# A hybrid convolution decoder step on one core: late spills cut in halves, quadrant loads moved behind them, merge sigmoids staged in PSUM

## What is computed

```python
z = rmsnorm(h, norm_g)
a_val, a_glu, a_gate, b_h, b_c, b_b, b_gate, m_a, m_b = split(z @ w_in)   # nine blocks of 1024 columns
c_a = layernorm(causal_dwconv(buf_a, a_val * sigmoid(a_glu), conv_a_w) + conv_a_b)   # width 31
y_a = silu(c_a) * silu(a_gate)
y_b = b_b * causal_dwconv(buf_b, b_c * b_h, conv_b_w) * silu(b_gate)                # width 3
merged = sigmoid(m_a) * (y_a @ w_pa) + sigmoid(m_b) * (y_b @ w_pb)
y = rmsnorm(h + merged @ w_out)
```

## Time and profile before

| what | us |
|---|---|
| median of 3 runs (1175.93 to 1176.99) | 1176.33 |
| the profiled execution's own time | 1175.6 |
| its span, first to last instruction | 1173.8 |
| TensorE matmul busy in it | 1055.5 |
| late units n = 2 to n = 10 (to slot 4) | 233.03 |

### The profile page before, as it was taken

How to read it: one execution, slowest core, us unless ns; L and a number is a source line. 1 busy time by engine, 2 the same in 40 slices (tenths; PEclk the granted TensorE clock), 3 DMA queues, 4 the chain that set the end, 5 groups by cost and what they waited for, 6 DMA issues and landing times.

```text
span 1173.8 us, 19871 instructions
## 1 busy us (share of the span) xinstructions
PE 1055.5 (90%) x7948; PEld 1024.7 (87%) x7948; DVE 762.7 (65%) x816; ACT 460.1 (39%) x694; POOL 601.6 (51%) x451
## 2 busy tenths in 40 slices
PE   4868999999999999999998888895966986997997
PEld 4868999999999999999998888895966976996885
DVE  5635979899999999898845436330661384646333
ACT  7334343433434444344344444461541252222221
POOL 2155666565656565665745555543754564545000
PEclk8888999999999999999999999888988988998999
DMA  7446575666656667565688879988669877764220
GB/s 258 107 118 139 129 196 128 181 153 164 164 146 171 157 162 173 143 174 144 160 245 223 236 207 271 282 238 285 168 190 282 226 187 213 198 235 163 91 90 37
DMA packets 217583, 212.24 MB, mean 181 GB/s; under 512 B 10799, under 2 KB 171055, under 8 KB 216452
## 3 DMA queue, kind: packets, MB, share of 16 engines
q1 hardware_dynamic: 192724, 165.88, 44.5%
q0 software_dynamic: 24768, 45.10, 21.4%
HBM read 131.83 MB, written 35.00 MB: 142 GB/s over the span
## 4 chain that ended last, share of the span: by engine, by line
PE 64%; DMA 12%; issue 5%; DVE 4%; POOL 4%; ACT 3%; SPq 2%; ACTq 0%; DVEq 0%; POOLq 0%
PE pp L1816 55%; PE pp L1968 8%; POOL wop L837 4%; DMA m_spill<-big 3%; DMA ring<-in_w_in_dram 2%; DMA ring<-ring 2%; DMA big<-mb_spill 2%; DVE big L1529 2%; DMA ga_spill<-big 1%; DVE big L1531 1%; SPq L433 1%; ACT xop L932 1%; ACT wop L906 1%; DMA mb_spill<-big 1%; DMA big<-yb_spill 1%
## 5 line engine op out<-in xcount | busy, mean ns | idle before, releaser
L1816 PE MATMUL pp<-xop,wop 128*128 128x262 f32 (+1 forms) x7224 | 913.6, 289 | 82.9 <-ACT big L1060 61.2
L1816 PEld LDWEIGHTS pp<-xop,wop 128*128 128x128 f32 x7224 | 906.4, 194 | 88.0 <-issue 82.9
L837 POOL TENSOR_TENSOR wop<-ring,wop 128x512 fp32r<-128x512 f32 (+1 forms) x262 | 455.2, 1745 | 367.5 <-ACT wop L906 367.1
L906 ACT ACTIVATE wop<-ring 128x512 fp32r<-128x512 f32 (+1 forms) x262 | 182.0, 698 | 271.5 <-PE pp L1816 258.1
L1512 DVE TENSOR_TENSOR big<-big,pp 128x524 f32<-128x524 f32 (+1 forms) x43 | 29.9, 694 | 121.6 <-PE pp L1816 120.8
L1432 DVE SCALAR_TENSOR_TENSOR big<-big,cst 128x513 f32<-128x513 f32 x112 | 104.7, 935 | 0.6
L1968 PE MATMUL pp<-xop,wop 128*128 128x512 f32 x384 | 91.3, 400 | 6.7 <-DVE wop L1766 6.7
L1968 PEld LDWEIGHTS pp<-xop,wop 128*128 128x128 f32 x384 | 73.4, 192 | 24.3 <-issue 6.9
L1443 DVE SCALAR_TENSOR_TENSOR spare<-big,tap_sum,spare 128x512 f32<-128x512 f32 x112 | 83.7, 748 | 0.3
L1432 DVE SCALAR_TENSOR_TENSOR spare<-big,cst,spare 128x512 f32<-128x512 f32 x112 | 83.6, 746 | 0.0
L1347 DVE TENSOR_TENSOR xop<-big,xop 128x2064 fp32r<-128x2064 f32 (+1 forms) x21 | 54.0, 2592 | 41.6 <-ACT xop L932 41.5
(11 more groups left out here) (119 smaller groups left out, 674.4 us busy)
## 6 DMA issues: line engine op xcount, KB each, us to landing
ring<-in_w_in_dram SPq DMA_DIRECT2D x249, 256.0 KB, 3.5
ring<-ring POOLq DMA_DIRECT2D x172, 256.0 KB, 4.5
big<-c_spill SPq DMA_DIRECT2D x16, 516.0 KB, 6.7
ring<-in_w_pb_dram SPq DMA_DIRECT2D x28, 256.0 KB, 4.2
ring<-in_w_pa_dram SPq DMA_DIRECT2D x28, 256.0 KB, 3.6
big<-yb_spill SPq DMA_DIRECT2D x5, 1032.0 KB, 11.3
big<-ya_spill SPq DMA_DIRECT2D x5, 1032.0 KB, 11.8
yb_spill<-big SPq DMA_DIRECT2D x8, 516.0 KB, 5.4
```

The lines of the kernel that those rows point to most:

```text
L837: G.tensor_tensor(wop[:, s0:s1, 1, :], raw, f(wop[:, s0:s1, 0, :]), ALU.subtract).then_inc(wlo, 1)
L906: A.activation(wop[:, s0:s1, 0, :], raw, ACT.Copy).then_inc(whi, 1)
L1816: last = T.matmul(out, wop[:, s, wp, P * k:P * (k + 1)], xop[s][:, xp, k, n * ch:n * (ch + 1)], start=(s in FRESH and k == 0 and m == 0), ...
```

## The change

1. Late units: the function on `g1` runs in halves (`act_late`) as soon as `c22` and `c12` have completed each, ahead of `act_last`. `spill_q` becomes `spill_q2` (second half, at the end of the unit's own SP body, behind `load_rb22`) and `spill_q1` (first half, in the next body right behind `load_u13`). `spill_p2` moves behind `load_u4`. `third_product` waits for the first half's spill, `fourth_product` for the second's. `freed` waits for `act_last`, now the fourth step.
2. pb: the spill of `g1` is cut the same way (`spill_pbq2`, `spill_pbq1`).
3. Quadrant loads: two stand behind the phase's `load_x22`/`load_sgb` place (after `load_u4` and the spills), two behind `load_u2`. `load_x22` stands ahead of `load_sgb` and `load_siga`. `x_high(p, 6)` moves behind `fourth_product`, `x_low(p, 6)` behind `c22`, and `x_sum(p, 1)` into the next unit, ahead of `c11`.
4. pb: ScalarE copies each loaded `sgb` piece into two PSUM banks (`sgc`, `stage_sigmoids`); DVE's product reads it from there, and the next `load_sgb` waits for that copy.

```diff
+        sgc = spare_pair[:, :, 0:CY]
...
-                sp.wait_ge(late_step, 3 * n + 3)
-                sp.dma_start(late_rows(n)[1], g1[:, META:ALL]).then_inc(lq_out, 16)
+            def spill_q2(n):
+                sp.wait_ge(late_step, 4 * n + 2)
+                sp.dma_start(late_rows(n)[1][:, HZ - META:TOK], g1[:, HZ:ALL]).then_inc(lq2_out, 16)
+            def spill_q1(n):
+                sp.wait_ge(late_step, 4 * n + 3)
+                sp.dma_start(late_rows(n)[1][:, 0:HZ - META], g1[:, META:HZ]).then_inc(lq1_out, 16)
...
                 if m == 0 and n == 0:
                     sp.wait_ge(lp1_out, 16 * LATES)
                     sp.wait_ge(lp2_out, 16 * LATES)
-                    sp.wait_ge(lq_out, 16 * LATES)
-                else:
-                    sp.wait_ge(pb_step, 4 * m + n)
+                    sp.wait_ge(lq1_out, 16 * LATES)
+                    sp.wait_ge(lq2_out, 16 * LATES)
+                else:
+                    sp.wait_ge(sgc_ready, 3 * m + n)
...
                 if last_n >= 0:
-                    spill_p2(last_n)
+                    spill_q1(last_n)
+                if last_kind == "pb":
+                    spill_pbq1(last_i)
...
-                if n == 9:
-                    for q in (2, 3, 0, 1):
-                        load_quad(1, q)
...
                 if last_n >= 0:
-                    spill_q(last_n)
+                    spill_p2(last_n)
...
                 if last_kind == "pb":
                     spill_pb2(last_i)
+                if u == NZ:
+                    load_x22(1)
+                if u == NPB:
+                    load_x22(2)
                 if kind == "pb":
                     load_sgb(i, 0)
                 if kind == "pa":
                     load_siga(i)
-                if u == NZ:
-                    load_x22(1)
-                if u == NPB:
-                    load_x22(2)
+                if n == 9:
+                    load_quad(1, 2)
+                    load_quad(1, 3)
+                if u == NZ + 1:
+                    load_quad(2, 2)
+                    load_quad(2, 3)
...
+            def stage_sigmoids(m, n):
+                act.wait_ge(sgb_in, 48 * m + 16 * (n + 1))
+                if n:
+                    act.wait_ge(pb_step, 4 * m + n)
+                else:
+                    wait(act, pb_step, 4 * m - 1)
+                A.activation(sgc, sgb[:, :].rearrange("p (c w) -> p c w", w=CY), ACT.Copy).then_inc(sgc_ready, 1)
+            def act_late(u, h):
+                act.wait_ge(ev, snap_at(u, 2 - h))
+                src = half(g1, u, h)
+                A.activation(src, src, ACT.Sigmoid if UNITS[u][0] == "mix" else ACT.Silu).then_inc(late_step, 1)
...
                     x_high(1, 0)
+                if kind == "pb":
+                    stage_sigmoids(i, 0)
                 if u == NZ:
                     x_high(1, 5)
...
                 act_first(u)
+                if kind == "pb":
+                    stage_sigmoids(i, 1)
...
+                if kind == "pb":
+                    stage_sigmoids(i, 2)
+                if n >= 0:
+                    act_late(u, 1)
                 if u == NZ - 1:
                     x_high(1, 3)
+                if n >= 0:
+                    act_late(u, 0)
...
-                    dve.wait_ge(sgb_in, 48 * i + 16)
-                    V.tensor_tensor(g3[:, 0:HY], g3[:, 0:HY], sgb[:, :], ALU.mult).then_inc(pb_step, 1)
+                    dve.wait_ge(sgc_ready, 3 * i + 1)
+                    V.tensor_tensor(half(g3, u, 0), half(g3, u, 0), sgc, ALU.mult).then_inc(pb_step, 1)
```

More of the change, by code:

```diff
@@ L513, in load_ga @@
                     if j % 2:
-                        sp.wait_ge(lq_out, done)
+                        sp.wait_ge(lq1_out, done)
+                        sp.wait_ge(lq2_out, done)
                     else:
@@ L560, in spill_pb1, with spill_pbq2, spill_pbq1 @@
                 sp.dma_start(mb_spill[:, 2 * m, 0:HY], g3[:, 0:HY]).then_inc(mb1_out, 16)
+            def spill_pbq2(m):
+                sp.wait_ge(pb_step, 4 * m + 2)
+                sp.dma_start(mb_spill[:, 2 * m + 1, HY:TOK], g1[:, HY:TOK]).then_inc(mbq2_out, 16)
+            def spill_pbq1(m):
+                sp.wait_ge(pb_step, 4 * m + 3)
+                sp.dma_start(mb_spill[:, 2 * m + 1, 0:HY], g1[:, 0:HY]).then_inc(mbq1_out, 16)
             def spill_pb2(m):
@@ L742, in _ @@
                     load_c(9)
+                if n == 9:
+                    load_quad(1, 0)
+                    load_quad(1, 1)
+                if u == NZ + 1:
+                    load_quad(2, 0)
+                    load_quad(2, 1)
                 if n == 5:
@@ L769, in _ @@
                     load_c(14)
+                if n >= 0:
+                    spill_q2(n)
                 if n == 8:
                     spill_ya(7)
+                if kind == "pb":
+                    spill_pbq2(i)
                 if u == LAST - 1:
@@ L1062, in fourth_product @@
             def fourth_product(u):
+                kind, i = UNITS[u]
+                n = late(u)
                 if u == 1:
                     act.wait_ge(xlo, X0[3])
+                elif n > 0:
+                    act.wait_ge(lq2_out, 16 * n)
+                elif kind == "pb":
+                    act.wait_ge(*((mbq2_out, 16 * i) if i else (lq2_out, 16 * LATES)))
+                elif kind == "pa":
+                    act.wait_ge(*((pa_step, 8 * i - 4) if i else (mbq2_out, 64)))
                 act.wait_ge(prod, prod_at(u, 3))
@@ L1274, in _ @@
                     w_hi(v, 3)
+                if u == NZ:
+                    x_high(1, 6)
+                if u == NPB:
+                    x_high(2, 6)
                 if n == 4:
@@ L1294, in _ @@
                     std_row(2)
+                if kind == "pb":
+                    stage_sigmoids(i, 2)
+                if n >= 0:
+                    act_late(u, 1)
                 if u == NZ - 1:
                     x_high(1, 3)
+                if n >= 0:
+                    act_late(u, 0)
+                if u == NZ - 1:
                     x_high(1, 4)
@@ L1536, in after_c22 @@
                     dve.wait_ge(ev, snap_at(u, 1))
-                    dve.wait_ge(sgb_in, 48 * i + 32)
-                    V.tensor_tensor(g1[:, HY:TOK], g1[:, HY:TOK], sgb[:, :], ALU.mult).then_inc(pb_step, 1)
+                    dve.wait_ge(sgc_ready, 3 * i + 2)
+                    V.tensor_tensor(half(g1, u, 1), half(g1, u, 1), sgc, ALU.mult).then_inc(pb_step, 1)
                 if kind == "pa" and i:
@@ L1560, in after_c12 @@
                     dve.wait_ge(ev, snap_at(u, 2))
-                    dve.wait_ge(sgb_in, 48 * i + 48)
-                    V.tensor_tensor(g1[:, 0:HY], g1[:, 0:HY], sgb[:, :], ALU.mult).then_inc(pb_step, 1)
+                    dve.wait_ge(sgc_ready, 3 * i + 3)
+                    V.tensor_tensor(half(g1, u, 0), half(g1, u, 0), sgc, ALU.mult).then_inc(pb_step, 1)
                 if kind == "pa":
@@ L1655, in _ @@
                     normalize_c(1)
+                if u == NZ - 1:
+                    x_sum(1, 1)
+                if u == NPB - 1:
+                    x_sum(2, 1)
                 if u == NZ:
@@ L1717, in _ @@
                     x_sum(2, 3)
+                if u == NZ:
+                    x_low(1, 6)
+                if u == NPB:
+                    x_low(2, 6)
                 c12(u)
@@ L1851, in freed @@
                 elif late(u - 1) >= 0:
-                    pe.wait_ge(late_step, 3 * late(u - 1) + 2)
+                    pe.wait_ge(late_step, 4 * late(u - 1) + 4)
                 elif kind == "pb":
```

45 lines of the change are left out of this document (16 added, 29 removed).

## The result

| | before | after |
|---|---|---|
| device time, median (us) | 1175.7 (1170.36 to 1181.28, 20 runs) | 1169.72 (1163.04 to 1177.25, 20 runs) |
| ratio, 95% interval | | 0.995 [0.993, 0.997] |
| profiled execution (us) | 1175.6 | 1170.91 |
| its span (us) | 1173.8 | 1169.1 |

The kernel became faster, by 6 us and not by the 43 that were forecast, and 1169.7 lies above the whole range. The profiled spans differ by 4.7. The profile after shows where the 43 went, so it is read in two halves: the late units, which gained, and phases pb and pa, which gave most of it back.

What follows compares the result with a forecast made beforehand. TensorE was taken to stall on late spills: about 47 us lost in the late units, 30.7 in pb and pa gaps. Terms 28 + 0 + 7 - 2 + 2 + 8 = 43 off 1176.3 gave 1133 us, range 1110 to 1158.

Steps and rivals of the forecast that it cites:

- What is late next: Late units, n = 2 to 10: with gaps closed, the DMA engines set the pace at a share of 0.95; gain 28 us.
- A: Late units: DMA engines are the next bound and halves cost in the queue; gain 11 us, time 1150, chance 0.20.
- Halves, n = 2 to 8: Late units: the first half's spill lands 3.5 us before the deadline, so six gaps (17.4 us) nearly close.
- rival D: Late units: halves land no sooner because `load_rb22` ahead waits for GpSimd; only n = 9 gains, 1163 us, chance 0.08.
- pb 0 to pb 3: The four pb units: old gaps close but staging copies delay some products; 0, +7, -2 and +2 us.
- pa 0: First pa unit: `third_product` stops waiting for the fifth quadrant, first merge comes after 25 us instead of 33.0; +8 us.
- rival C: pb units: ScalarE's queue holds up TensorE at each of 12 stagings, 3.9 us each; 1178 us and up, chance 0.04.
- nine of the twelve have a slot or more of cover: pb units: argument against a slower kernel, that nine of 12 staging copies have at least a slot of slack.

Runs made afterwards that it cites:

- thin loads: The changed kernel with the layer norm's second loads of `c` and its gate loads cut to 64 of 1032 columns: 1159.71 us, ratio 0.9853.

## Why the prediction was wrong

**What is late next (28 forecast, 12 measured).** This step took a DMA share of 0.95 for all nine units. It came to 0.88: 0.81 up to n = 5, 0.94 from there to n = 9, 0.98 in the unit after. The bytes were right (0.88 x 220.90 = 194 us of busy engines, 193 forecast); that one share could hold over stretches with different limits was not. Two waits keep units near 23 us, and the prediction had both as rivals. From n = 5 on one is A's: a unit takes 23.25 us at 0.94, and thin loads bring it to 20.5. Full engines are not all of it: with an earlier `load_u4` one run went at 21.7 us a unit (86.9 / 4), with a share of 1.00 over 94 us. The 1.5 us between the two are put down to the wait of the next paragraph; that is argued from its lines. A's time for the late units, 11 us, was nearly the one measured, but its reason, halves that cost in the queue, did not show: the engines were busy for 0.83 x 235.57 = 196 us before and 194 after, with one more transfer in each unit. The Trainium skill's fixed cost of about 2 us ("DMA: Bandwidth & Descriptors", "Anatomy of one DMA"; the section is on DMAs that GpSimd issues, and SyncE issues these spills) would, as an estimate, be 9 x 2 = 18 us if the engines paid it here; the trace shows that they did not.

**Halves, n = 2 to 8.** The working took 1800 KB at 254 GB/s, counted from a `load_rb22` at the unit's start. That was the wrong anchor. The chain of the changed kernel around the same n = 7:

```profile
738.23 3.17 DMA ring<-in_w_in_dram
...
746.72 7.00 DMA ga_spill<-big
...
753.74 0.62 ACT big L1091
```

By the way of the earlier trace rows this unit began at 754.49 - 4.11 - 4 x 2.92 = 738.7. `load_rb22` (L431) was issued at 743.95, 5.3 us later, where it had come 0.1 us after the start before. It had waited for GpSimd's `w_lo` (L868), and `load_u2` ahead of it for a sum of weights to land. Behind both, the first half left at 746.72 and took 7.00 us: landed 15.0 us after the unit's start, deadline 10.9. SP's waits from 738 to 747 us:

```profile
SPq L423 <- DMA ring<-ring: 7.0, 1, 7.0
SPq L431 <- POOL wop L868: 3.7, 1, 3.7
```

From one `load_rb22` to the next it is 24.8 us, as before. The units could start earlier, the weights that gate SP's queue could not, and the half spill stands behind them. This is rival D's mechanism, which the prediction put at 0.08 because the nine transfers of the earlier trace rows showed a queue and no wait. The wait stood just ahead of the first of the nine. SP's waits before, from 738 to 756 us, L427 being the `load_rb22` of 747.40:

```profile
SPq L427 <- POOL wop L837: 6.4, 1, 6.4
```

What holds n = 2 and n = 3 back in particular (1.50 and 3.53 us even with thin loads) was not settled.

**pb 0 to pb 3 (+7 forecast, -10 measured).** From start to start the four units took 32.0, 33.1, 20.3 and 28.5 us before and 39.0, 29.6, 25.2 and 30.3 after: -7.0, +3.5, -4.9 and -1.8 against 0, +7, -2 and +2. The 28.5 of pb 3 end at pa 0's start, 967.21. The prediction put that at 965.5, a fifth of the way through the 16.80 us of the earlier trace rows, but the first of these five slots ran at the lower clock (the window of it, columns as in the earlier trace rows):

```profile
962.14:967.21 5.07, 5.07 (x25) 5.07 (x26) 4.57 (x5) 5.07 (x4) 2.06 (x1) 0.53 0.39 90
```

The mechanism, a copy that holds up `third_product` or `fourth_product`, was named in pb 0 to 2 and as rival C; its size was wrong. The sentence that fell is "nine of the twelve have a slot or more of cover". All four units have a gap before slot 5, and undoing the copies gives 16.8 us, 1.4 for each of the twelve (C wanted 3.9). Right were the gap of pb 0 before slot 4 (near 9 forecast, 10.23 measured, through `sgb` and the copy) and pb 1's change from a gap before slot 4 to one before slot 5 (4.6 and 6.75). Left out was the second gap of pb 0 (4.16), from the wait of 6.92 us for its second piece.

**pa 0 (+8 forecast, +2.5 measured).** No gap before slot 4, as forecast, and the first merge came 28.8 us after the unit's start (25 forecast). Before it was 31.3, not the 33.0 that the prediction counted from 965.5. The merge waits for the load of the old rows (L602). It was issued 20.0 us after the unit's start instead of 25.0, so 5 us earlier where 9 were booked, behind a sum of weights that `load_u2` (L424) waited for, and it took 8.7 us instead of 6.3. The chain of the changed kernel:

```profile
975.14 7.84 DMA ring<-ring
...
983.04 0.37 SPq L424
...
983.59 6.25 DMA big<-mb_spill
```

TensorE's gap there has a step that was not costed either: `x_high(2, 6)` stands behind `w_hi`(3), which waited 5.60 us for a sum of weights, and `x_low` after it took 4.74 us, so slot 6 waited 8.23. ScalarE's and VectorE's timelines of the changed kernel:

```profile
981.60 1.06 ACT L937 ACTIVATE wop<-ring 128x1024 fp32r<-128x1024 f32 x1 [5.60 <-DMA ring<-ring]
982.56 1.91 ACT L963 ACTIVATE xop<-big 128x2064 fp32r<-128x2064 f32 x1
```

```profile
984.50 4.74 DVE L1407 TENSOR_TENSOR xop<-big,xop 128x2064 fp32r<-128x2064 f32 x1 [5.58 <-ACT xop L963]
...
992.41 0.69 DVE L1589 TENSOR_TENSOR big<-big 128x516 f32<-128x516 f32 x1 [2.57 <-issue]
```

That the order of these two opens the gap before slot 6 is shown by the run with the order changed (3.55 us without staging, then 0.14). The merge waits for the old rows all the same, and no gain in the total was resolved.

**The sum.** 12.2 - 10.2 + 2.5, with 1.6 gained ahead of the late units and 1.4 lost behind the first merge, makes the 4.7 us between the two profiles. The pb units, where the staging is, came out 17 us under the forecast, the late units 16 and pa 0 5.5.

## What to carry to other kernels

An instruction that waits for a DMA belongs, in an in-order queue, behind everything that doesn't need its data: the same twelve copies of 0.6 us cost 22 to 24 us more in one place than in another. Before a closed gap is booked as a gain, ask which gate comes next in each stretch by itself: sum the transfers' busy time there, and look at what released the first transfer of a queue before calling the queue the cause. And price a change's parts alone: here one part gained 13 us and another gave 17 away.

## What the runs showed of the hardware

The DMA engines held a share of 0.97 for 94 us in one run and of 1.00, at 292 GB/s, in another. Cutting a spill of 516 KB into halves added no busy time that can be seen (196 us before, 194 after). VectorE's subtraction of 128x2064 elements, which takes 2.8 us in the mean of two in the earlier trace rows, took 4.74 in pa 0; why was not tried.
